# Two gated branch projections and an output projection, each rewritten as seven half-size products with added operand sums

## The reference

```python
a = gmlp_spatial_gating(z_u, z_v, gmlp_ln_g[i], gmlp_ln_b[i], gmlp_w_s[i], gmlp_b_s[i])
b = forgetting_attention(q, k, v, f_logit, b_f[i])
y_a = jnp.einsum('bsc,cd->bsd', a, w_branch_a[i])
y_b = jnp.einsum('bsc,cd->bsd', b, w_branch_b[i])
merged = gate_a * y_a + gate_b * y_b
x = x + jnp.einsum('bsd,de->bse', merged, w_out[i])
h2 = rmsnorm_2(x, norm_ffn_g[i])
up = jnp.einsum('bsd,df->bsf', h2, w_up[i])
```

## Time and profile before

| what | value |
|---|---|
| median of 3 runs | 1606.81 us (1606.65 to 1607.15) |
| profiled execution, its own time | 1607.59 us |
| its span in the trace | 1605.9 us |
| PE busy | 1587.6 us, 99% of the span |
| PEld busy | 1305.8 us |
| DVE busy | 1078.5 us, 67% |
| ACT busy | 710.6 us, 44% |
| POOL busy | 181.5 us, 11% |
| granted TensorE clock | 1.00 of full speed over nearly all of the span |

### The profile page before, as it was taken

The page is one execution under the profiler, slowest core; times in us unless marked ns, Lnnn a source line. Parts: engine busy times, 40 slices in busy tenths (PEclk is TensorE's granted clock), DMA queues, the critical chain, the costliest instruction groups (busy, mean ns, idle before and its releaser), DMA issues.

```text
span 1605.9 us, 20446 instructions
## 1 busy us (share of the span) xinstructions
PE 1587.6 (99%) x8187; PEld 1305.8 (81%) x8187; DVE 1078.5 (67%) x1494; ACT 710.6 (44%) x1018; POOL 181.5 (11%) x263
## 2 busy tenths in 40 slices
PE   9999999999999999999999999999999999999998
PEld 7877777888888888878788887888888888888888
DVE  6756788669393865657744477445566876878857
ACT  6524575545252524415662156342334443443544
POOL 0001055000000000024500255000000000000000
PEclk9999999999999999999999999999999999999999
DMA  5233321264757522331022211322237347344221
GB/s 191 80 106 125 123 95 53 79 210 131 236 132 235 131 106 94 116 138 72 27 105 83 101 53 53 136 101 105 93 143 262 102 135 238 93 154 158 105 106 53
DMA packets 32894, 195.14 MB, mean 122 GB/s; under 512 B 4320, under 2 KB 6816, under 8 KB 11296
## 3 DMA queue, kind: packets, MB, share of 16 engines
q1 hardware_dynamic: 25056, 160.20, 27.0%
q0 software_dynamic: 2880, 20.97, 6.8%
q10 hardware_dynamic: 4864, 12.66, 2.2%
HBM read 187.50 MB, written 6.32 MB: 121 GB/s over the span
## 4 chain that ended last, share of the span: by engine, by line
PE 87%; DVE 7%; issue 2%; ACT 2%; POOL 1%; DMA 0%; DVEq 0%; ACTq 0%; POOLq 0%
PE bank L767 20%; PE bank L769 19%; PE bank L768 19%; PE bank L1189 3%; PE bank L1190 3%; PE bank L1191 3%; PE bank L815 3%; PE bank L817 3%; PE bank L816 3%; PE bank L1000 1%; PE bank L775 1%; PE bank L985 1%; DVE w_lo L2370 1%; PE bank L744 1%; DVE up_c L2668 1%
## 5 line engine op out<-in xcount | busy, mean ns | idle before, releaser
L767 PE MATMUL bank<-a_hi,w_hi 128*128 128x512 f32 x1160 | 456.8, 394 | 0.6 <-DVE x L2030 0.6
L769 PE MATMUL bank<-a_hi,w_lo 128*128 128x512 f32 x1160 | 452.0, 390 | 0.0
L768 PE MATMUL bank<-a_lo,w_hi 128*128 128x512 f32 x1160 | 451.6, 389 | 0.0
L1375 ACT ACTIVATE w_hi<-w_raw 128x2048 fp32r<-128x2048 f32 x95 | 181.3, 1908 | 184.5 <-DMA w_raw<-in_strips 182.7
L769 PEld LDWEIGHTS bank<-a_hi,w_lo 128*128 128x128 f32 x1160 | 217.8, 188 | 45.9
L767 PEld LDWEIGHTS bank<-a_hi,w_hi 128*128 128x128 f32 x1160 | 217.9, 188 | 45.3 <-issue 2.3
L768 PEld LDWEIGHTS bank<-a_lo,w_hi 128*128 128x128 f32 x1160 | 218.0, 188 | 43.0 <-issue 0.2
L1951 DVE TENSOR_TENSOR w_lo<-w_raw,w_hi 128x2048 fp32r<-128x2048 f32 x92 | 210.9, 2293 | 54.4 <-ACT w_hi L1375 54.3
L1189 PE MATMUL bank<-w_hi,t_hi 128*128 128x512 f32 x280 | 109.3, 390 | 0.1
L1191 PE MATMUL bank<-w_hi,t_lo 128*128 128x512 f32 x280 | 109.0, 389 | 0.0
L1190 PE MATMUL bank<-w_lo,t_hi 128*128 128x512 f32 x280 | 109.0, 389 | 0.0
(11 more groups left out here) (364 smaller groups left out, 2658.0 us busy)
## 6 DMA issues: line engine op xcount, KB each, us to landing
w_raw<-in_strips SPq DMA_DIRECT2D x107, 1024.0 KB, 4.8
a_part<-in_parts SPq DMA_DIRECT2D x25, 1024.0 KB, 7.4
a_part<-in_parts POOLq DMA_DIRECT2D x20, 1024.0 KB, 9.1
spare<-in_parts SPq DMA_DIRECT2D x5, 1024.0 KB, 15.0
spare<-in_strips SPq DMA_DIRECT2D x5, 1024.0 KB, 4.9
seg_in<-cum_kept ACTq DMA_DIRECT2D x16, 256.0 KB, 3.5
x_kept<-x ACTq DMA_DIRECT2D x2, 2048.0 KB, 9.2
x<-x_kept SPq DMA_DIRECT2D x2, 2048.0 KB, 9.9
```

The lines of the kernel that those rows point to most:

```text
L767: mm(ps[:, :], w_hi[slot][:, k, cols], hi[:, k, :], start=(k == 0), stop=False)
L768: mm(ps[:, :], w_hi[slot][:, k, cols], lo[:, k, :], start=False, stop=False)
L769: return mm(ps[:, :], w_lo[slot][:, k, cols], hi[:, k, :], start=False, stop=(k == kt - 1))
L1375: run(w_hi[j], w_raw[j], ACT.Copy).then_inc(hi_split, 1)
```

## The change

`branch_b`, `branch_a` and `out2` (the list `FOLD`, with f = 0, 1, 2) each become 7 products. The 1024 x 1024 weight is cut into four quarters of 512 x 512 and the activations into four quarters (`quad`: 4 feature tiles by 256 positions). Each product multiplies one quarter-sized weight (a raw quarter or a sum) with one quarter-sized activation (raw or a sum): 4 column tiles by 4 feature tiles by 3 matmuls of 256 columns, in two halves of 24. A strip is now one of the 7 operands of a phase, still 1 MB, so the three phases have 21 strips in place of 12.

The weight sums are made in DRAM ahead of time, four sums for each of the three weights (`pre`). SP copies a quarter DRAM to DRAM behind each of 12 strips from `ff2_3` on, and POOL adds another quarter with an adding transfer: six of them in attention call "2a", six in the phases `u` and `qk2b`. A product's strip is then one plain transfer into one of two buffers (`fold_raw`), which SP issues when the strip two before it has been split (`low_ready`). The activation sums (`fold_sums`) are on DVE. Partial products are kept by ACT (`keep_first`, `keep_second`) and combined by DVE (`keep_sums`, `take`, `add_known`). For strip (2, 0), the first of `out2`, the low part is made by POOL and not by DVE. x is read back in two halves inside `branch_a`/`out2` and not in `gate_a`.

```diff
-PHASES += [("branch_b", 4), ("branch_a", 4), ("out2", 4)]
+FOLD = ["branch_b", "branch_a", "out2"]
+QUADS = [(0, 0), (1, 0), (0, 1), (1, 1)]
+FOLD_BANK = [4, 6, 4, 6, 2, 6, 2]
+FOLD_QUAD = [0, 1, 2, 0, 1, 3, 2]
+FOLD_SOURCE = [(0, 0), 0, (1, 0), 2, 1, 3, (1, 1)]
+PRE_SUMS = [(0, 1), (0, 0), (0, 0), (1, 0)]
+PRE_COPIES = [(kind, f) for kind in range(4) for f in range(3)]
+PHASES += [(name, 7) for name in FOLD]
...
+                    elif n == 15:
+                        sp_eng.wait_ge(*low_ready(s - 3))
+                    elif n != 1:
+                        sp_eng.wait_ge(*low_ready(s - 2))
+                    f, i = FOLDED[s]
+                    source = FOLD_SOURCE[i]
+                    sp_eng.dma_start(flat(fold_at(s)), fold_part(f, source) if i in (0, 2, 6) else pre[source, f]).then_inc(fold_loaded[n % 3], 16)
...
+                if 0 <= s - FIRST["ff2_3"] - 1 < len(PRE_COPIES):
+                    kind, f = PRE_COPIES[s - FIRST["ff2_3"] - 1]
+                    sp_eng.dma_start(pre[kind, f], fold_part(f, PRE_SUMS[kind])).then_inc(copied[kind // 2], 16)
...
+                    if call == "2a" and n % TT == 2 and 1 <= n // TT <= 6:
+                        add_part(*PRE_COPIES[n // TT - 1])
...
+            s = FIRST[FOLD[2]]
+            pool.wait_ge(hi_split, s)
+            pool.tensor_tensor(w_lo[s % W_SLOTS], fold_at(s), w_hi[s % W_SLOTS].bitcast(F32), ALU.subtract).then_inc(pool_split, 1)
...
-            stream("branch_b", feature_k, B, ready=lambda k: pe.wait_ge(att_lo, 4 + k + 1))
-            stream("branch_a", feature_k, A, ready=wait_tiles(amix_lo))
-            stream("out2", feature_k, B, ready=wait_tiles(m_lo))
...
+            def folded(f):
+                for i in range(7):
+                    s = FIRST[FOLD[f]] + i
+                    slot, (t, k0) = s % W_SLOTS, QUADS[FOLD_QUAD[i]]
+                    hi, lo = quad(fold_hi[f], t, k0), quad(fold_lo[f], t, k0)
+                    pe.wait_ge(*low_ready(s))
...
+                    for h in range(2):
+                        fold_bank(f, i, h)
+                        for e in range(2):
+                            ps = bank[FOLD_BANK[i] + h][:, e * (T // 2):(e + 1) * (T // 2)]
+                            cols = slice((2 * h + e) * P, (2 * h + e + 1) * P)
+                            for k in range(W4):
+                                mm(ps, w_hi4[slot][:, k, cols], hi[:, k, :], start=(e == 0 and k == 0 and i in (0, 1, 4)), stop=False, skip_group_check=True)
+                                mm(ps, w_hi4[slot][:, k, cols], lo[:, k, :], start=False, stop=False, skip_group_check=True)
+                                last = mm(ps, w_lo4[slot][:, k, cols], hi[:, k, :], start=False, stop=(k == W4 - 1), skip_group_check=True)
+                        last.then_inc(unit_done, 1)
...
+            def high_strip(f, i):
+                s = FIRST[FOLD[f]] + i
+                act.wait_ge(fold_loaded[(s - FIRST[FOLD[0]]) % 3], fold_count(s))
+                act.wait_ge(unit_done, 2 * (s - W_SLOTS) + 2)
+                run(w_hi[s % W_SLOTS], fold_at(s), ACT.Copy).then_inc(hi_split, 1)
...
+            def keep_sums(f):
+                src, e0 = fold_src[f], EVAC0[FOLD[f]]
+                for h in range(2):
+                    product_ready(f, 3, h)
+                    dve.wait_ge(snapped, SNAPPED0 + 4 * f + h + 1)
+                    v.tensor_tensor(quad(src, 0, 0, h), halves(6 + h), quad(fold_kept[f], 1, 1, h), ALU.add).then_inc(dve_evac, 1)
...
+                    fold_do(v.tensor_tensor(fold_q[h], quad(src, 0, 0, h), fold_q[h], ALU.subtract))
+            def take(f, i, j, step, at):
+                for h in range(2):
+                    product_ready(f, step, h)
...
+                if f == 0:
+                    fold_do(v.tensor_tensor(total, total, new, ALU.mult))
+                else:
+                    fold_do(v.tensor_tensor(new, new, gate, ALU.mult))
+                    v.tensor_tensor(total, total, new, ALU.add).then_inc(merged_ready, 1)
...
+            take_22 = lambda f: take(f, 1, 1, 4, 4)
+            take_21 = lambda f: take(f, 1, 0, 5, 6)
+            take_12 = lambda f: take(f, 0, 1, 6, 8)
...
+            low_strip(0, 5)
+            low_four(1, 3)
+            fold_sums(1, 2)
+            fold_sums(1, 3)
+            take_22(0)
+            low_strip(0, 6)
...
+            take_21(2)
+            lo(FIRST["up0"])
+            for m in range(4):
                 low("ffn2", m, gains[:, 5, :], (a_hi, a_lo))
                 add_square("ffn2", m)
+            take_12(2)
+            lo(FIRST["up0"] + 1)
+            for m in range(4, KT):
+                low("ffn2", m, gains[:, 5, :], (a_hi, a_lo))
+                add_square("ffn2", m)
```

More of the change, by code:

```diff
@@ L1784, in _, with sigmoids @@
             attention("2b", "gate_b", None)
-            def sigmoids(phase, where):
-                for j in range(KT):
+            def sigmoids(phase, where, first, last):
+                for j in range(first, last):
                     act.wait_ge(dve_evac, EVAC0[phase] + j + 1)
@@ new lines, in keep_second @@
+            def keep_second(f):
+                if f:
+                    act.wait_ge(dve_evac, EVAC0[FOLD[f - 1]] + 10)
+                for h in range(2):
+                    act.wait_ge(unit_done, 2 * FIRST[FOLD[f]] + 2 + h + 1)
+                    run(fold_q[h], halves(6 + h), ACT.Copy).then_inc(snapped, 1)
+            sigmoids("gate_b", merged, 0, KT)
+            hi(FIRST["gate_a"] + 2)
+            high_four(0, 0)
+            high_four(0, 1)
+            hi(FIRST["gate_a"] + 3)
+            high_four(0, 2)
@@ new lines, in _, with fold_do, take_first @@
+            fold_n = [FOLD_STEP0]
+            def fold_do(ins):
+                fold_n[0] += 1
+                ins.then_inc(fold_step, 1)
+                dve.wait_ge(fold_step, fold_n[0])
+            def take_first(f):
+                if f < 2:
+                    dve.wait_ge(gated, KT * (f + 1))
+                where, op = ((merged3, ALU.mult), (gate3, ALU.mult), (x, ALU.add))[f]
+                for h in range(2):
+                    product_ready(f, 2, h)
+                    part = quad(where, 0, 0, h)
+                    v.tensor_tensor(part, part, halves(4 + h), op).then_inc(dve_evac, 1)
+                if f == 1:
+                    dve.wait_ge(dve_evac, EVAC0[FOLD[1]] + 2)
+                    v.tensor_tensor(quad(merged3, 0, 0), quad(merged3, 0, 0), quad(gate3, 0, 0), ALU.add).then_inc(merged_ready, 1)
@@ L2641, in _ @@
-            dve.wait_ge(x_loaded[0], 48)
-            for m in range(KT):
-                add_x("out2", m, m)
+                if 1 <= j <= 4:
+                    low_four(0, j - 1)
+                if j in (4, 6):
+                    low_strip(0, j // 2 - 2)
+                if j in (0, 3, 5, 7):
+                    fold_sums(0, (0, 3, 5, 7).index(j))
+            fold_sums(1, 0)
+            low_four(1, 0)
+            low_strip(0, 2)
+            low_three(0, 0)
+            low_four(1, 1)
@@ new lines, in _ @@
+            low_strip(1, 2)
+            low_three(1, 0)
+            low_strip(1, 3)
+            low_three(1, 1)
+            low_strip(1, 4)
+            take_first(1)
+            low_three(1, 2)
+            low_four(2, 0)
+            keep_sums(1)
+            low_strip(1, 5)
+            take_22(1)
+            low_strip(1, 6)
+            take_21(1)
+            fold_sums(2, 0)
+            low_strip(2, 1)
+            low_four(2, 1)
+            low_strip(2, 2)
+            take_12(1)
```

348 lines of the change are left out of this document (276 added, 72 removed).

## The result

| | before | changed |
|---|---|---|
| median | 1607.15 us (16 runs, 1606.58 to 1607.75) | 1610.59 us (16 runs, 1607.70 to 1612.65) |
| ratio, 95% interval | | 1.0022 (1.0015 to 1.0029) |
| profiled execution, span | 1607.59, 1605.9 | 1608.64, 1606.7 |
| mean granted clock of one execution | 1.0 in the profiled one; 0.999 to 1.0 in 78 of the 79 timed beside the experiments | 0.998 (3 runs), 0.997 (1), 0.996 (4), 0.995 (8) |

The change made the kernel slower by 3.4 us, 0.22%. The forecast was 1.0 us faster (1605.8, from 1606.81). Two things are off: the profiled execution by 2.0 us (1606.6 was worked out, 1608.64 came), and the median lies 2.0 us above the profiled execution.

The account below looks back on a forecast made before the run. The prediction took PE's matmul time as the bound. Savings -9.6, stalls +7.9, restart +0.4 and attention +0.3 gave -1.0 us, so a median of 1605.8 us from 1606.8, range 1600.8 to 1610.8.

Parts of the forecast that it names:

- the list: Hand-made schedule of the DVE, ACT, PE, SP and POOL queues side by side; its three PE stalls sum to 7.9 us.
- What the change saves: Three phases: 336 matmuls of 120.0 ns each phase in place of 192 of 226.7 ns, saving 9.6 us.
- Stall 1: Before product 6 of `branch_b`: DVE reaches strip (0, 6) only after two sums and `take_22(0)`; PE waits 1.2 us.
- Stall 2: Before product 6 of `branch_a`: POOL's operation holds DVE's last add of `take_22(1)`, delaying strip (1, 6); PE waits 4.6 us.
- the bounds: Price of POOL's 2048-column operation on strip (2, 0): between 3.9 and 5.8 us, 4.8 taken.
- Stall 3: Start of `up0`: DVE makes the low part of feature tile 4 late in its queue; PE stands 2.1 us.
- Restarts: Weight load, otherwise hidden, when PE restarts after a stall: 0.4 us added, for the last stall only.
- The attention: POOL's six issues in "2a" cost 0 to 5.2 us; 0.3 taken, as POOL waited 39.0 us in 14 waits there.
- Rival 3: Attention "2a": all of POOL's issues there delay PE, +4.9 us on the forecast, 1610.7 us; chance 0.07.
- Rival 1: `branch_a`: POOL's operation does not hold DVE or lets it pass between pieces, 4.6 us earlier, 1601.2 us; chance 0.22.
- Rival 2: Three phases: loading into the two raw buffers sets the pace, ending 2.0 or 3.5 us later, up to 1610.3; chance 0.17.
- Rival 4: DVE's entries run better than listed, with cheaper evacuations and the first and third stalls gone: 1602.5 us; chance 0.09.

Follow-up runs that it names:

- the new queue: The changed kernel with strip (2, 0) on DVE and another order of DVE's queue in the three phases and `up0`: 1607.64 us, ratio 1.0003.

## Why the prediction was wrong

It named the stalls and got the sign wrong. **The step that failed is the sum**, -9.6 + 7.9 + 0.4 + 0.3: it has no term for the granted clock, which the prediction took as 1.00 throughout and said it had not priced. In the profiled execution that term is 1.6 us, more than the 1.0 us that was forecast as the gain. The rest of its distance of 2.0 us is small: stalls and restarts 0.4 below the list, the attention 0.2 above its term, and 0.6 not placed. The further 2.0 us between profiled execution and median follow the mean clocks, as said below.

- **What the change saves, -9.6.** Right: starts of 256 columns are 120 ns apart in all three phases wherever PE did not wait and the clock was full.
- **Stall 1, 1.2 us.** Measured 1.2, by the queue that was named; with strip (0, 6) moved up it went.
- **Stall 2, 4.6 us.** Measured 4.1. The list had POOL start first and hold the last add of `take_22(1)`. The add was just ahead, so it took its usual time, only the strip was held, and POOL's record became 5.52 us. From the add's end it is 4.43, a little under the 4.8 taken. So the choice between the bounds was nearly right, and the order of the two starts was not. The Trainium skill, GPSIMD Engine Reference, section 3.1, gives 4497 ns for such an operation; the trace agrees with it by the 4.43 to 4.49 us from the end of DVE's operation, and does not if the whole 5.52 us are counted.
- **Stall 3, 2.1 us.** Measured 2.1.
- **Restarts, 0.4.** Each of the three gaps is 0.16 us longer than its wait and one distance of starts, 0.5 in sum.
- **The clock behind the stalls, 0 in the sum.** 1.6 us in the profiled execution. Two fillings of the 4.1 us with useless matmuls show that it is PE's idleness that brings it and not DVE or POOL at work: in both the clock there stays at 1.00, where it fell behind the same wait in all three profiles that leave it unfilled.
- **The attention, 0.3 us.** `branch_b` started 0.5 us later in the profiled execution. The effect on the median is not settled: moving the adds away lowered it by 2.2 us in the changed kernel and by 1.5 with the stall filled, and raised it by 0.3 with the new queue; putting them into the kernel before raised it by 1.0, with an interval that takes in no change. Rival 3 had priced it at up to 5.2 by POOL's issues alone; its mechanism, PE waiting longer for POOL's rows, was there at a small part of that. The 39.0 us in which POOL waits were the wrong witness: they lie in 14 waits, and on the path are those few rows for which PE waits.
- **The median.** Among the 16 executions those with a mean clock of 0.998 average 1608.7, those with 0.995 average 1611.7: 1.0 us for each 0.001, one short stretch at the lower level. The profiled execution had one such stretch within the span's middle; most others, by their means, had three or four. The forecast for the median carried over the distance of before, whose profile has no such stretch there. Three places are known from profiles (the table above); which fell in a given timed execution, and where a fourth is, no profile shows. So this part of the account goes by the means alone.
- **Rival 1** (without the exclusion) did not happen, and its 1601.2 was doubtful: I had taken the stall out of the list and not run the list on. With POOL's operation gone the span was 2.3 us shorter and not 4.6, since the wait before product 2 of `out2` took the rest. That kernel has DVE make the strip too, and the one with strip (1, 6) first has the same wait with DVE held elsewhere, so what POOL's operation without the exclusion would have given no run shows. **Rival 2** did not happen as a wait of PE: the medians of the landings are 4.8 and 5.0 us. But strip (2, 2), issued at 1133.96 right behind a half of x, took 8.1 us, and DVE stood 2.15 us for it. In the changed kernel no wait of PE followed; with the strip on DVE 0.79 us of the same kind stand ahead of the new wait. **Rival 4** did not happen either.

Open is why the wait in "2a" is 0.9 to 1.1 us in some profiled executions and 1.4 in others of the same attention code.

## What to carry to other kernels

A stall on PE can cost more than its length where the engine was at full clock before: price it with the matmuls behind it at the lower level, and expect executions to differ, since not each one loses the clock. When engines go from half busy to full, take a stall out of the list only by running the list to its end; here the waits that were removed came back in part as later ones until the order of the whole queue fitted, and then DVE was busy for 98% of the window of `out2`. Where two engines exclude each other, ask which of them starts first, since a record of either may hold its wait for the other. An engine's large waiting time says nothing of cover if the few rows that PE waits for are among what is delayed.

## What was not expected of the hardware

- POOL's subtraction of 128 x 2048 float32 from two on-chip inputs took 5.52 to 5.60 us in six kernels, each time begun just behind the start of a two-input operation of DVE, and 4.43 to 4.49 us from the end of that one, where DVE takes 2.29. In eight pieces it was 745 ns for the shortest piece and 1.7 us for the median piece beside a busy DVE; five of DVE's own operations then ran 0.4 to 0.5 us long.
- In 13 profiles the lower clock followed each unfilled wait of PE from 3.2 to 4.8 us, four of seven of 2.1 us, and in the attention each of 1.4 us and none of 0.7 to 1.1, where PE is not full around the wait either. While it lasted 18 matmuls of 256 columns lost 1.6 us.
- The waits of 2.2, 2.3 and 1.9 us in `out2` were not followed by it in the three profiles that have them.
